# One stage for the input norm and the projections, one 264-column product for values and index weights, index scores between the projections

## The chip, the cores and the metric

The kernel runs on one core of one Trainium2 chip. The metric is the device time of one execution in microseconds (us), lower is better. TensorE is called PE in the profile, VectorE DVE, ScalarE ACT, GpSimd POOL, and SP is the engine that issues the loads.

## The reference, cut to what matters

One inference step of a two-layer encoder for 1024 new tokens of one stream and 32 tokens of a running one (1056 tokens, 1024 features, all float32). Layer 0 is attention in which an indexer picks 256 keys for each query; layer 1 is a gated linear recurrence. The change touches the beginning of layer 0 only:

```python
hn = rmsnorm(h, norm_w[0])
p = hn @ w_in                     # 1024 x 3720
q, k, v, z, qi, ki, wi = split_cols(p, [1024, 256, 256, 1024, 1024, 128, 8])
q, k, qi, ki = rope(q), rope(k), rope(qi), rope(ki)
idx_logits = einsum('bthd,bsd->bths', qi, ki)                    # 8 index heads
score = einsum('bth,bths->bts', wi * IDX_SCALE, relu(idx_logits))
_, sel = lax.top_k(score, n_sel)                                 # 256 (sample: 136) keys
```

After it come softmax attention over the selected keys, the output product, the recurrence and a final norm, which stay as they are. `v` is an output too.

## The kernel before

Tokens lie in nine tiles of 128 (the last has the 32 sample tokens). Products with weights are computed in split precision: each operand is a high part (a cast to fp32r) and a low part (the rest), and `product` (L181) adds three passes for each of the 8 slices of 1024 features, so one product is 24 matmuls.

**`input_norm` (L258)**, a block of its own. Per token tile: load x (three buffers; the load of tile t waits for tile t - 3 to be scaled), ACT squares and sums (L314), POOL turns the sum into a factor (`norm_stats_pool`, L239 and L242), DVE scales (L339), PE transposes eight 128x128 pieces (L365), and the transposed rows are multiplied by the norm weight and split into `hn_hi` and `hn_lo` (`split_normed` L173 and L176 on DVE, L305 on ACT). From t = 5 on ACT and POOL also split one of the first three weight tiles (`split_weights_hi` L208, `split_weights_lo` L215), POOL after the factor of the same t.

**`attention_project` (L370)**, the next block, goes through a list of units written out by hand. For the 30 weight tiles of 128 columns in the order KI, WI, QI0 to QI7, K0, K1, V0, V1, then Z and Q in turn, there are three units each (352 tokens a unit, weights stationary). The WI tile computes 128 columns for the eight index weights that it needs; they are transposed back by PE (L554) and copied by DVE (L748). V0 and V1 are done together in nine units, one for each token tile, tokens stationary and 256 columns moving. The index scores of all eight heads are one block of 96 units ahead of K1 (L560). A score unit is one float32 matmul of 272 to 512 columns, an ACT relu into one of two buffers (L607), and a DVE multiply-add into `score` (L758; L754 for head 0). PE may be four units ahead of their reader (four PSUM banks), ACT two units ahead of DVE:

```python
if i >= 4: pe.wait_ge(act_read, n_act[i - 3])
if s >= 2: act.wait_ge(scored, s - 1)
```

A rope unit has two ACT copies (L588, L589), a DVE product with cos (L739) and two POOL products and sums with sin (L641, L630). There are three slots for weights. SP loads tile c when PE is through with tile c - 3 (L464), and ACT and POOL split it after the unit that this line names:

```python
after.setdefault(min(last_of_tile[c - SLOTS] + 2, last_of_tile[c - 1]), []).append(c)
```

Once all scores are there, DVE searches each query's threshold bit by bit: `begin` and then 31 times propose, count over seven tiles (L714) and decide (L725, L726). It starts behind the first rope unit after the scores (K1's first), goes on between the last ropes and then by itself (L760 to L772). The attention block starts when all engines are done.

Of the kernel before, what the change touches and what calls it, by code (L numbers as in the profile page):

```python
# [16 lines left out]
ALU = mybir.AluOpType  # L17
# [8 lines left out]
P = 128  # L26
D = 1024
# [17 lines left out]
WI_TILE = WI0 + IH - P  # L45
W_SLOTS = 3

TILES = [KI0, WI_TILE] + [QI0 + P * i for i in range(IH)] + [K0 + P * i for i in range(2 * KVH)]
# [39 lines left out]
def build(nc, io):  # L88
    with ExitStack() as ctx:
# [37 lines left out]
        S["open"] = space("open_mask", [P, 3 * P])  # L127
        w_at = space.at
# [24 lines left out]
        input_norm(nc, S)  # L153
        attention_project(nc, S, space)
# [102 lines left out]

def input_norm(nc, S):  # L258

    io, sem, ps = S["io"], S["sem"], S["ps"]  # L260
    stats, half, ident, columns = S["stats"], S["half"], S["ident"], S["columns"]
    const_in, x_in = sem("const_in"), [sem(f"x_in{i}") for i in range(3)]
# [3 lines left out]
    act_hi_done = sem("hn_hi0_act")  # L266
# [6 lines left out]
    junk = space("junk", [P, D])  # L273
    with nc.Block() as block:  # L274
        @block.sync
        def _(sp):
            sp.dma_start(ident[:], io["ident"]).then_inc(const_in, 16)
            sp.dma_start(by_row[0:2 * KT], io["norm_w"].rearrange("l (k p) -> (l k) p", p=P)).then_inc(const_in, 16)
            sp.dma_start(by_row[2 * KT:3 * KT], io["rec_lb_logits"].rearrange("l (k p) -> (l k) p", p=P)).then_inc(const_in, 16)
            sp.dma_start(by_row[3 * KT:4 * KT], io["rec_gnorm_w"][0]).then_inc(const_in, 16)  # L280
            for t in range(NT):
                if t >= 3:
                    sp.wait_ge(xn_ready, t - 2)
                    sp.wait_ge(squares_ready, t - 2)
                sp.dma_start(xin[0:rows(t), t % 3, :], token_rows(io, t)).then_inc(x_in[t % 3], 16)

                c = t - FIRST_WEIGHT
                if 0 <= c < W_SLOTS:
                    sp.dma_start(S["w_raw"][:, c], w_in[:, :, TILES[c]:TILES[c] + P]).then_inc(S["raw_in"][c], 16)
            for name in ("cos", "sin", "limits"):  # L290
                sp.dma_start(S[name][:], io[name]).then_inc(S["tables_in"], 16)
            ck = cached_keys(S["score"])
            sp.dma_start(ck[:, :, 0:256], io["cache_k"][0, 0].rearrange("(b p) h d -> p b (h d)", p=P)).then_inc(S["cache_in"], 16)
            sp.dma_start(ck[:, :, 256:384], io["cache_kidx"][0, 0].rearrange("(b p) d -> p b d", p=P)).then_inc(S["cache_in"], 16)
            sp.dma_start(S["cv"][:], io["cache_v"][0, 0].rearrange("(b p) h d -> p b (h d)", p=P)).then_inc(S["cache_in"], 16)

        @block.scalar
        def _(act):
            def upper(t):

                act.wait_ge(columns_out, 1)
                act.wait_ge(tr_ready, 2 * t + 2)
                r = rows(t)
                for k in range(4):
                    last = act.activation(S["hn_hi"][:, 4 + k, span(t)], ps[2 * (t % 2) + 1][:, k * P:k * P + r],  # L305
                                          ACT.Copy, scale=columns[:, 0, 4 + k:5 + k])
                last.then_inc(act_hi_done, 1)

            for t in range(NT):
                r = rows(t)  # L310
                act.wait_ge(x_in[t % 3], 16 * (t // 3 + 1))
                if t:
                    act.wait_ge(squares_ready, t)
                act.activation(junk[0:r], xin[0:r, t % 3, :], ACT.Square,  # L314
                               accum_out=stats[0:r, 0, t:t + 1]).then_inc(squares_ready, 1)
                if t >= 2:
                    upper(t - 2)
# [1505 lines left out]
```

## Time and profile before

| | |
|---|---|
| median of three runs | 1551.94 us (1550.73 to 1554.93) |
| span of the profiled execution | 1547.9 us, 2.8 to 7.0 us under the three runs |
| busy in the span | PE 1402.9, DVE 965.9, ACT 560.5, POOL 508.8 us |
| input norm | 0 to 40 us |
| projections, scores, search | 40 to 492 us |
| everything after (not touched) | 492 to 1548 us |

The profiled execution has no time of its own beside its span; the runs' median lies 4.0 us above it. Times in the rows count from the start of the span.

### The profile page before, as it was taken

Reading aid. Unit: us, or ns where it says so; the run is one execution under the profiler, and the core shown is the slowest. Engines: PE = TensorE matmul, PEld = TensorE weight load, DVE = VectorE, ACT = ScalarE, POOL = GpSimd, SP = SyncE. Lnnn points to the kernel's source line nnn. Section 1 sums busy time; section 2 is a strip of 40 time slices with the busy share of each in tenths; the row PEclk is TensorE's granted clock in tenths of the full one; section 3 lists DMA queues with packets and bytes.
Section 4 is the critical chain, followed back from the end, with each engine's and each line's share of the span. In section 5 each row is a group of like instructions: output and inputs, shape, how many; then the busy total and the mean of one; then the engine's idle time right before and its main releaser. Section 6 shows DMA issues by size and latency. Waiting matters only on the chain. (4 is left out here: it accounts for less than half of the span.)

```text
span 1547.9 us, 21333 instructions
## 1 busy us (share of the span) xinstructions
PE 1402.9 (91%) x8109; PEld 1224.0 (79%) x8109; DVE 965.9 (62%) x1864; ACT 560.5 (36%) x1004; POOL 508.8 (33%) x404
## 2 busy tenths in 40 slices
PE   4999999999993899999979999999999999925898
PEld 3999647999992455548869999999999999914686
DVE  7011488999998989744550466475665566596332
ACT  6233463333322555541121444342525253340111
POOL 4276402355541001100020364544536163363000
PEclk9999999999996999999999999999999999957899
DMA  6121100232211410002231111010211110500221
GB/s 217 28 55 41 28 1 15 78 95 85 65 53 42 149 28 14 4 28 82 82 89 43 56 29 47 28 61 20 61 41 42 36 40 20 193 4 1 82 99 62
DMA packets 96180, 86.78 MB, mean 56 GB/s; under 512 B 4528, under 2 KB 84272, under 8 KB 96080
## 3 DMA queue, kind: packets, MB, share of 16 engines
q1 hardware_dynamic: 94448, 80.60, 16.9%
q0 software_dynamic: 1632, 4.82, 0.9%
q8 instruction: 66, 1.08, 0.3%
q14 instruction: 34, 0.28, 0.1%
HBM read 65.43 MB, written 19.97 MB: 55 GB/s over the span
## 5 line engine op out<-in xcount | busy, mean ns | idle before, releaser
L186 PE MATMUL bank<-hn_hi,rw_hi 128*128 128x352 f32 x768 | 250.3, 326 | 2.9 <-PEq L1009 2.9
L186 PE MATMUL bank<-hn_hi,rw_lo 128*128 128x352 f32 x768 | 247.2, 322 | 0.0
L186 PE MATMUL bank<-hn_lo,rw_hi 128*128 128x352 f32 x768 | 246.9, 322 | 0.0
L186 PE MATMUL bank<-hn_hi,w_hi 128*128 128x352 f32 x672 | 218.9, 326 | 3.6 <-PEq L274 3.6
L186 PE MATMUL bank<-hn_lo,w_hi 128*128 128x352 f32 x672 | 216.5, 322 | 0.0
L186 PE MATMUL bank<-hn_hi,w_lo 128*128 128x352 f32 x672 | 216.4, 322 | 0.0
L714 DVE TENSOR_SCALAR_CACHE_REDUCE marks<-score,bits 128x384 bf16<-128x384 f32 (+6 forms) x217 | 185.1, 917 | 3.7
L186 PEld LDWEIGHTS bank<-hn_hi,rw_hi 128*128 128x128 f32 x768 | 144.6, 188 | 4.6 <-POOL rw_lo L1145 3.1
L186 PEld LDWEIGHTS bank<-hn_lo,rw_hi 128*128 128x128 f32 x768 | 145.0, 189 | 0.0
L186 PEld LDWEIGHTS bank<-hn_hi,rw_lo 128*128 128x128 f32 x768 | 144.6, 188 | 0.0
L186 PEld LDWEIGHTS bank<-hn_hi,w_hi 128*128 128x128 f32 x672 | 127.0, 189 | 4.3 <-issue 3.7
L186 PEld LDWEIGHTS bank<-hn_lo,w_hi 128*128 128x128 f32 x672 | 127.2, 189 | 0.0
L186 PEld LDWEIGHTS bank<-hn_hi,w_lo 128*128 128x128 f32 x672 | 126.8, 189 | 0.0
L641 POOL TENSOR_TENSOR swapped<-swapped,sin 128x352 f32<-128x352 f32 x57 | 54.0, 947 | 187.8 <-ACT swapped L589 122.1
L1573 DVE TENSOR_TENSOR levels<-levels,q_rec 128x528 f32<-128x528 f32 (+1 forms) x48 | 101.4, 2177 | 1.9 <-ACT levels L1409 1.9
L843 PE MATMUL wide<-kT,q_tile 128*128 128x512 f32 (+3 forms) x192 | 75.4, 506 | 27.1 <-DMA q_tile<-q_rotated 26.9
L239 POOL TENSOR_SCALAR stats<-stats 128x1 f32<-128x1 f32 (+1 forms) x27 | 7.4, 273 | 279.4 <-ACT junk L1116 162.6
L1328 PE MATMUL wide<-levels 128*128 128x128 f32 (+1 forms) x832 | 98.2, 274 | 0.6
L1328 PEld LDWEIGHTS wide<-levels 128*128 128x128 f32 (+1 forms) x832 | 92.7, 185 | 6.0 <-issue 0.9
L1145 POOL TENSOR_TENSOR rw_lo<-rw_raw,rw_hi 128x1024 fp32r<-128x1024 f32 x32 | 76.0, 2386 | 59.6 <-ACT rw_hi L1138 59.5
L215 POOL TENSOR_TENSOR w_lo<-w_raw,w_hi 128x1024 fp32r<-128x1024 f32 x30 | 71.7, 2390 | 50.4 <-ACT w_hi L208 50.3
L843 PEld LDWEIGHTS wide<-kT,q_tile 128*128 128x128 f32 x192 | 36.6, 202 | 65.1 <-issue 34.2
(221 smaller groups left out, 2823.2 us busy)
## 6 DMA issues: line engine op xcount, KB each, us to landing
rw_raw<-in_rec_w_in SPq DMA_DIRECT2D x32, 512.0 KB, 4.1
w_raw<-in_att_w_in SPq DMA_DIRECT2D x30, 512.0 KB, 3.9
q_rotated<-relu SPq DMA_DIRECT2D x24, 176.0 KB, 1.9
xin<-in_x_prompt SPq DMA_DIRECT2D x8, 512.0 KB, 4.2
q_tile<-q_rotated SPq DMA_DIRECT2D x8, 512.0 KB, 3.7
wo_raw<-in_att_w_out SPq DMA_DIRECT2D x4, 1024.0 KB, 9.1
x_again<-in_x_prompt SPq DMA_DIRECT2D x8, 512.0 KB, 4.0
residual<-h_rows SPq DMA_DIRECT2D x8, 512.0 KB, 2.9
```

Source lines behind the costliest of these rows:

```text
L186: last = pe.matmul(out, l, r, start=n == 0, stop=n == len(passes) - 1)
L215: pool.tensor_tensor(S["w_lo"][:, slot], S["w_raw"][:, slot], S["w_hi"][:, slot].bitcast(F32), ALU.subtract).then_inc(S["w_lo_done"], 1)
L239: pool.tensor_scalar(stats[0:r, 1, t:t + 1], stats[0:r, 0, t:t + 1], 1.0 / D, EPS, ALU.mult, ALU.add).then_inc(pool_order, 1)
L641: pool.tensor_tensor(swapped[:, r % 3, :], swapped[:, r % 3, :], sin[:, part * CW:(part + 1) * CW], ALU.mult).then_inc(sin_done, 1)
L714: step(dve.tensor_scalar(marks[0:r, i % 2, 0:keys(t)], tile(i, t), bound, 0.0, op, ALU.add, accum_out=counts[0:r, first + i:first + i + 1]))
L843: last = pe.matmul(logits[0:rows(t), i % 2, a:e], q[:, t % 2, h, 0:rows(t)], src[:, h // GROUP, a:e], start=True, stop=True)
L1145: pool.tensor_tensor(S["rw_lo"][:, slot], S["rw_raw"][:, slot], S["rw_hi"][:, slot].bitcast(F32), ALU.subtract).then_inc(S["rec_lo_done"], 1)
L1328: last = pe.matmul(out[:, 0:r], left, right, start=True, stop=True)
L1573: dve.tensor_tensor(x, x, level_view(q[:, slot], m)[:, :, 1, :], ALU.mult).then_inc(q_scaled, 1)
```

## The change

The two blocks become one: each engine runs the instructions of the norm and goes on with the projections without a meeting of the engines. The norm weight is multiplied in on DVE together with the scale, from a copy that a load spreads over 128 partitions. Values and index weights are one product per token tile (tokens stationary, 264 columns moving), done in the norm's loop one tile behind the transposes. Their weights come in four loads ahead of x1, two of them with pieces of eight floats, and are split by ACT (after the first tile) and DVE. The WI tile, the V units and the transposes of the index weights are gone; 27 weight tiles stay. The index scores are no longer one block: the 12 units of head h stand ahead of weight tile QI(h+2), and those of heads 6 and 7 ahead of K0. The search starts behind K0's first unit, so K0 and K1 both lie behind the scores.

```diff
-TILES = [KI0, WI_TILE] + [QI0 + P * i for i in range(IH)] + [K0 + P * i for i in range(2 * KVH)]
+TILES = [KI0] + [QI0 + P * i for i in range(IH)] + [K0 + P * i for i in range(KVH)]
...
+    first, later = input_norm(nc, S), attention_project(nc, S)
+    with nc.Block() as block:
+        @block.sync
+        def _(sp):
+            first["sync"](sp)
+            later["sync"](sp)
...
+    def sync(sp):
+        sp.dma_start(ident[:], io["ident"]).then_inc(ident_in, 16)
+        for t in range(NT):
+            if t >= 3:
+                sp.wait_ge(xn_ready, t - 2)
+                sp.wait_ge(squares_ready, t - 2)
+            sp.dma_start(xin[0:rows(t), t % 3, :], token_rows(io, t)).then_inc(x_in[t % 3], 16)
+            if t == 0:
+                sp.dma_start(norm_w, io["norm_w"][0].partition_broadcast(P)).then_inc(norm_in, 16)
                 for g in range(2):
+                    ks = slice(4 * g, 4 * g + 4)
+                    sp.dma_start(wv_raw[:, ks, 0:KV], w_in[:, ks, V0:V0 + KV]).then_inc(wv_in[g], 16)
+                    sp.dma_start(wv_raw[:, ks, KV:VW], w_in[:, ks, WI0:WI0 + IH]).then_inc(wv_in[g], 16)
...
+    def scalar(act):
+        def upper(t):
+            for g in range(2):
+                act.wait_ge(tr_ready, 2 * t + g + 1)
+                act.copy(S["hn_hi"][:, 4 * g:4 * g + 4, span(t)], transposed(t, g)).then_inc(hi_done, 1)
+
+        def read_v(t):
+            act.wait_ge(v_ready, t + 1)
+            src = wide[token_block(t)[1], 2 + t % 2, :]
+            act.copy(S["v"][0:rows(t), t, :], src[:, 0:KV])
+            act.mul(S["wi"][0:rows(t), t, :], src[:, KV:VW], IDX_SCALE).then_inc(v_read, 1)
+
+        for t in range(NT):
+            r = rows(t)
+            act.wait_ge(x_in[t % 3], 16 * (t // 3 + 1))
...
+            act.activation(junk[0:r], xin[0:r, t % 3, :], ACT.Square,
+                           accum_out=stats[0:r, 0, t:t + 1]).then_inc(squares_ready, 1)
+            if t >= 1:
+                upper(t - 1)
+            if t == 1:
+                for g in range(2):
+                    ks = slice(4 * g, 4 * g + 4)
+                    act.wait_ge(wv_in[g], 32)
+                    act.copy(wv_hi[:, ks, :], wv_raw[:, ks, :]).then_inc(wv_hi_done, 1)
+            if t >= 3:
+                read_v(t - 3)
+            if 0 <= t - FIRST_WEIGHT - 2 < W_SLOTS:
+                split_weights_hi(act, S, t - FIRST_WEIGHT - 2)
...
+    def vector(dve):
+        def scale(t):
...
+            dve.scalar_tensor_tensor(xn[0:r, t % 2, :], xin[0:r, t % 3, :], stats[0:r, 2, t:t + 1],
+                                     norm_w[0:r], ALU.mult, ALU.mult).then_inc(xn_ready, 1)
+
+        dve.wait_ge(norm_in, 16)
+        scale(0)
+        for t in range(NT):
+            if t + 1 < NT:
+                scale(t + 1)
+            for g in range(2):
+                dve.wait_ge(hi_done, 2 * t + g + 1)
+                at = slice(4 * g, 4 * g + 4)
+                dve.tensor_tensor(S["hn_lo"][:, at, span(t)], transposed(t, g),
+                                  S["hn_hi"][:, at, span(t)].bitcast(F32), ALU.subtract).then_inc(lo_done, 1)
+            if t == 0:
+                for g in range(2):
+                    ks = slice(4 * g, 4 * g + 4)
+                    dve.wait_ge(wv_hi_done, g + 1)
+                    dve.tensor_tensor(wv_lo[:, ks, :], wv_raw[:, ks, :], wv_hi[:, ks, :].bitcast(F32),
+                                      ALU.subtract).then_inc(wv_lo_done, 1)
...
+            if t >= 1:
+                m = t - 1
+                pe.wait_ge(lo_done, 2 * m + 2)
+                if m == 0:
+                    pe.wait_ge(wv_lo_done, 2)
+                if m >= 2:
+                    pe.wait_ge(v_read, m - 1)
+                product(pe, wide[:, 2 + m % 2, 0:VW],
+                        [lambda k, x=x: x[:, k, token_block(m)[0]] for x in (S["hn_hi"], S["hn_lo"])],
+                        [lambda k, x=x: x[:, k, :] for x in (wv_hi, wv_lo)]).then_inc(v_ready, 1)
...
+    def head_scores(h):
+        return [("score", h, piece, t) for t in itiles for piece in range((keys(t) + 511) // 512)]
+
     units = []
     for c, col in enumerate(tiles):
-        if col == K0 + P:
-            for t in itiles:
-                for piece in range((keys(t) + 511) // 512):
-                    units += [("score", h, piece, t) for h in range(IH)]
...
+        if QI0 + 2 * P <= col < KI0:
+            units += head_scores((col - QI0) // P - 2)
+        if col == K0:
+            units += head_scores(IH - 2) + head_scores(IH - 1)
...
+                    if part == 0 and t == itiles[0]:
+                        pe.wait_ge(rope_done, 3 * (c + 2))
...
-                if kind != "score" and n_score[i] > 0:
+                if kind != "score" and n_score[i] == n_score[N]:
```

The `product`, `split_weights_hi`, `split_weights_lo` and `norm_stats_pool` that it calls are those of before.

## Rows read from the trace of the kernel before

**Rows 1.** The page, part 2: busy tenths in 40 slices of 38.7 us.

```profile
PE   4999999999993899999979999999999999925898
...
DVE  7011488999998989744550466475665566596332
...
PEclk9999999999996999999999999999999999957899
```

**Rows 2.** Windows by stage: start:end, length, busy us (instructions) by engine, clock, DMA share, GB/s.

```profile
40.00:170.00 130.00, 130.00 (x805) 129.76 (x805) 15.22 (x29) 39.28 (x74) 75.22 (x71) 1.00 0.15 41
...
174.00:244.00 70.00, 69.63 (x193) 31.23 (x193) 57.04 (x92) 46.46 (x94) 2.40 (x2) 0.98 0.00 1
...
250.00:470.00 220.00, 218.16 (x1431) 217.31 (x1430) 213.39 (x509) 67.24 (x133) 105.00 (x90) 1.00 0.24 69
470.00:492.00 22.00, 0.00 (x0) 0.00 (x0) 21.26 (x57) 1.16 (x3) 3.77 (x5) 0.55 0.07 25
```

**Rows 3.** Timeline, end of the search: start us, us, engine, line, operation, tiles.

```profile
485.05 0.17 DVE L725 TENSOR_TENSOR bits<-counts,select_state 128x7 uint32<-128x7 f32 x1
...
491.76 0.17 DVE L725 TENSOR_TENSOR bits<-counts,select_state 128x7 uint32<-128x7 f32 x1
```

**Rows 4.** Timeline, start of the search behind K1's first unit.

```profile
248.12 0.45 ACT L588 COPY swapped<-bank 64x352 f32<-64x352 f32 x1 [2.05 <-PE bank L186]
...
249.05 0.52 DVE L739 TENSOR_TENSOR kT<-bank,cos 128x352 f32<-128x352 f32 x1 [2.28 <-ACT swapped L589]
...
249.53 0.07 DVE L684 MEMSET counts<- 128x14 f32 x1
```

**Rows 5.** Timeline, input norm: squares of tiles 0 and 2; a split, the factor behind it.

```profile
5.71 1.06 ACT L314 ACTIVATE junk<-xin 128x1024 f32<-128x1024 f32 x1 [3.70 <-DMA xin<-in_x_prompt]
...
8.96 1.06 ACT L314 ACTIVATE junk<-xin 128x1024 f32<-128x1024 f32 x1 [0.84 <-DMA xin<-in_x_prompt]
...
25.30 2.36 POOL L215 TENSOR_TENSOR w_lo<-w_raw,w_hi 128x1024 fp32r<-128x1024 f32 x1
...
27.75 0.51 POOL L239 TENSOR_SCALAR stats<-stats 128x1 f32<-128x1 f32 x1
```

**Rows 6.** Timeline: twelve transposes at full clock; copies of two V units in a row.

```profile
53.92 1.39 PEld L512 LDWEIGHTS wide<-ident,score 128*128 128x128 f32 x12
...
258.59 0.37 ACT L601 COPY v<-bank 128x256 f32<-128x256 f32 x1 [1.94 <-PE bank L186]
...
261.45 0.37 ACT L601 COPY v<-bank 128x256 f32<-128x256 f32 x1 [2.48 <-PE bank L186]
```

**Rows 7.** Groups by line and shape, last stage: busy us, mean ns.

```profile
L1738 DVE SCALAR_TENSOR_TENSOR y<-h_again,stats,final_w 128x1024 f32<-128x1024 f32 x8 | 10.3, 1285 | 17.5 <-POOL stats L242 17.5
```

**Rows 8.** Windows of 5 us: cold start of the projections; one weight load of 512 KB.

```profile
40.00:45.00 5.00, 5.00 (x17) 5.00 (x18) 0.00 (x0) 0.00 (x0) 0.59 (x3) 1.00 0.02 3
...
255.00:260.00 5.00, 5.00 (x43) 5.00 (x42) 4.79 (x14) 1.27 (x3) 0.94 (x1) 1.00 0.40 108
```

**Rows 9.** The page, part 6: loads of weight tiles, KB each, us to landing.

```profile
w_raw<-in_att_w_in SPq DMA_DIRECT2D x30, 512.0 KB, 3.9
```

**Rows 10.** Timeline, first score units: a weight split meets a score.

```profile
176.57 1.04 ACT L208 CAST w_hi<-w_raw 128x1024 fp32r<-128x1024 f32 x1
...
177.69 2.35 POOL L215 TENSOR_TENSOR w_lo<-w_raw,w_hi 128x1024 fp32r<-128x1024 f32 x1 [3.63 <-ACT w_hi L208]
...
178.03 2.42 DVE L758 SCALAR_TENSOR_TENSOR score<-relu,wi,score 128x384 f32<-128x384 f32 x1 [0.70 <-ACT relu L607]
```

**Rows 11.** Timeline: runs of seven scores on DVE, 512 and 272 columns.

```profile
184.78 5.89 DVE L758 SCALAR_TENSOR_TENSOR score<-relu,wi,score 128x512 f32<-128x512 f32 x7 [0.24 <-ACT relu L607]
...
237.82 4.05 DVE L758 SCALAR_TENSOR_TENSOR score<-relu,wi,score 32x272 f32<-32x272 f32 x7 [0.25 <-ACT relu L607]
```

**Rows 12.** Timeline: weight loads of two float32 records of 512 columns, full clock.

```profile
560.74 0.19 PEld L843 LDWEIGHTS wide<-kT,q_tile 128*128 128x128 f32 x1 [0.24 <-issue]
...
561.17 0.19 PEld L843 LDWEIGHTS wide<-kT,q_tile 128*128 128x128 f32 x1 [0.24 <-issue]
```

More of the change, by code:

```diff
@@ L127, in build @@
         S["open"] = space("open_mask", [P, 3 * P])
+        v_at = space.at - (3 * P + sum(keys(t) for t in range(2, NT)) - PAST // P * 384) * 4
+        S["wv_raw"] = Space(nc, v_at)("wv_raw", [P, KT, VW])
+        S["wv_lo"] = Space(nc, v_at)("wv_lo", [P, KT, VW], F32R)
         w_at = space.at
@@ new lines, in transposed @@
+    def transposed(t, g):
+        return ps[2 * (t % 2) + g][:].rearrange("p (k q) -> p k q", k=4)[:, :, 0:rows(t)]
+    def scalar(act):
[11 more added lines that the diff above has]
+            act.wait_ge(x_in[t % 3], 16 * (t // 3 + 1))
+            if t:
+                act.wait_ge(squares_ready, t)
+            act.activation(junk[0:r], xin[0:r, t % 3, :], ACT.Square,
[11 more added lines that the diff above has]
+                split_weights_hi(act, S, t - FIRST_WEIGHT - 2)
+        upper(NT - 1)
+        for t in range(NT - 3, NT):
+            read_v(t)
@@ L358, in _, with tensor @@
+    def tensor(pe):
+        pe.wait_ge(ident_in, 16)
+        for t in range(NT + 1):
+            if t < NT:
                 r = rows(t)
@@ L414, in attention_project @@
     n_score = [sum(u[0] == "score" for u in units[:i]) for i in range(N + 1)]
-    last_wi = max(i for i, u in enumerate(units) if u[0] == "wi")
     first_score = next(i for i, u in enumerate(units) if u[0] == "score")
     last_of_tile = {u[1]: i for i, u in enumerate(units) if u[0] != "score"}
-    second_v = tiles.index(V0) + 1
-    last_of_tile[second_v] = last_of_tile[second_v - 1]
-    assert (second_v - 1) % SLOTS + 1 == second_v % SLOTS
     after = {}
@@ L425, in attention_project @@
         after.setdefault(min(last_of_tile[c - SLOTS] + 2, last_of_tile[c - 1]), []).append(c)
-    v_last = max(i for i, u in enumerate(units) if u[0] == "v")
-    rows_before = {v_last + 4 + 3 * t: t for t in range(NT)}
+    first_gate = min(i for i, u in enumerate(units) if u[0] == "gate")
+    rows_before = {first_gate + 3 + 3 * t: t for t in range(NT)}
     def rotated(i):
@@ L457, in attention_project, with sync @@
     ck = cached_keys(score)
-    wiT = score[0:DEC, 2048:2048 + T]
-    with nc.Block() as block:
-        @block.sync
-        def _(sp):
+    if True:
+        def sync(sp):
             def load(c):
@@ L655, in _, with vector @@
             add_sine()
-        @block.vector
-        def _(dve):
+        def vector(dve):
             n_order = 0
```

206 lines of the change are left out of this document (81 added, 125 removed).

## The prediction, made before the changed kernel was run

> **What bounds the kernel now.** I read the slices first [rows 1]: PE is busy nearly everywhere except at the start and in the thirteenth slice, where it idles, the clock column dips and DVE is full. So the end of the projection block belongs to DVE. The windows say it exactly [rows 2]: from 470 to 492 PE does nothing while DVE works 21.3 of 22 us. The timeline shows what it does there: whole bits of the search, 6.71 us from decision to decision, the last at 491.8 [rows 3], and the next block starts behind it. Going back, DVE is 213 of 220 us busy from 250 to 470 [rows 2]: the search is one unbroken run from 249.5 [rows 4], and nothing that PE does beside it counts. So the figure to forecast is not PE's total work. It is **the time at which the search begins**, and that is the time at which K1's first unit comes through: PE began it one unit (3.8 us) before ACT's copy at 248.1, at 244.2, and the search starts 5.3 us after that [rows 4].
>
> What lies ahead of it: 40 us of norm; 33 units from 40 to 170; four us for the index weights and a wait; the score block, 70 us for 96 units [rows 2]. 805 records less 12 cache transposes and one beyond the end are 792 matmuls, 33 units of 24; without 1.4 us of transposes [rows 6] and 2.3 us of cold start (17 matmuls in the first 5 us, where 0.159 us each would give 31 [rows 8]) a unit is 126.3 / 33 = 3.82 us. In the score block DVE sets the pace: seven scores of 512 columns take 5.89 us, seven of 272 take 4.05 [rows 11], which is 0.84 and 0.58 each, 1.08 ns for each further column. A head has 12 pieces and 4768 columns: 12 x 0.58 + 1504 x 0.00108 = 8.6 us, with the gaps 70 / 8 = 8.8. PE needs less: two records for each score, a record of 512 columns 0.43 us [rows 12], so 1.68 ns a column and 8.0 us a head.
>
> **The change part by part.**
>
> *Removed ahead of the search:* the WI tile and K0's move behind the scores, 6 units x 3.82 = 22.9 us; the 4 us from 170 to 174; the norm's 40 us and the 2.3 us of cold start, which come back below in another form. The V units and K1 were behind the start of the search, under DVE's cover: V's 9 x 2.86 us [rows 6] leave PE there, but PE already had 22 us of idle time at the end [rows 2], so that removal is worth nothing. Now the same work stands ahead of the search. This is the main thing against the change.
>
> *The first stage.* The x loads landed at 5.7 (tile 0) and 9.0 (tile 2) [rows 5], 1.6 us for each 512 KB. Three small loads go from the front, so I put x0 at 4.5. Ahead of x1 now stand the spread norm weight (512 KB, 1.6 us) and the weights of V (1.06 MB, 3.3 us) with 1024 pieces of 32 bytes. For those pieces I have no row. Below they cost nothing beyond their bytes; a weight load is 1024 pieces of 512 bytes and keeps the 16 engines 0.40 x 5 = 2.0 us busy [rows 8]. I take 2.0, being nearest in count, and 4.0 as the upper end. x1 lands at 4.5 + 1.6 + 3.3 + 2.0 + 1.6 = 13.0. Behind it hang, on ACT: squares (1.15 with the read of the sum), the two copies of tile 0 (1.15, an estimate from the 0.37 us for 256 columns [rows 6]), two casts of V's weights (2.1, from 1.04 for 1024 columns [rows 10]), to 17.4. On DVE: the scale of tile 1 with two SBUF inputs, which takes 1.285 us in the last stage [rows 7]; two low parts (1.4); two low parts of V's weights (2.5, in the size of the same row). The first product can start at about 20.3. It runs cold: 17 matmuls of 352 columns in 5 us [rows 8] are 0.22 us for 264 columns, 5.3 us in all, to 25.6. That repays the cold start saved at 40.
>
> After that PE has, per tile, eight transposes (8 x 1.39 / 12 = 0.93) and a product of 24 (2.86 x 264 / 256 = 2.95) [rows 6], 3.9 us, and less transposing for the last: 25.6 + 8 x 3.9 - 0.7 = 56.1. In the tiles where weights are split, POOL's factor waits for the 2.36 us split ahead of it [rows 5], then come the 1.3 us scale and 1.4 us of low parts on DVE. Laid out in time, three tiles take about 4.5 us in place of 3.9: projections start at **57.5**, range 55 to 62. Against 42.3 (40 and the cold start) that is 15.2 us later.
>
> *The scores between projections.* Here the intended gain is PE's 8.0 in place of DVE's 8.8 us a head, since DVE's lag is made up under the next rope units. But the rule for splits ("two units after the tile that frees the slot") was harmless with units of 3.8 us, and now the two units are scores. Take X as the end of the last rope unit. The slot becomes free at X and its load lands 3.9 us later [rows 9]. ACT does two relus (to 2.3), then stands before the cast until X + 4.05, and ends it at 5.15 (the cast takes 1.04 [rows 10]). PE has its four banks of lead, used up at 3.85. Relus go on at 5.65, but POOL's split runs from 5.25 to 7.6, and the third score wants to start on DVE at 5.65. What happens then stands in the trace: a score that arrived 0.34 us behind the start of such a split took 2.42 us in place of 0.7, and ended 0.4 us behind POOL's end [rows 10]. So the third score ends at 7.95; ACT may be only two ahead, so PE's seventh and eighth score pass, but the ninth waits until 8.6; from there all go at DVE's pace. PE may start the next rope unit when the ninth is read: with scores ending at 8.6, 9.3, 10.05 and 10.85, at **11.6 us**, not 8.0. DVE ends at 14.5, ahead of the next rope at 15.4, so nothing is carried over. Head 0 has a cheaper first operation: 11.1. Heads 6 and 7 stand together and share a split: 11.6 + 8.8 = 20.4. The sum is 11.1 + 5 x 11.6 + 20.4 = 89.5 us, against 70 before: 19.5 us more.
>
> The Trainium skill ("SBUF — State Buffer", section "Who interferes with whom") says that a DVE instruction with two SBUF inputs and a GpSimd instruction that reads SBUF exclude each other for the whole instruction; the 2.42 us agree. By it the new scale with two inputs can be held up by a split in the same way. Its page "DMA: Bandwidth & Descriptors" (Specifications) puts the smallest transfer at line rate at 512 bytes, which speaks for a price of the 32-byte pieces; no row here shows one.
>
> *Sum.* K0's first unit starts at 57.5 + 27 x 3.82 (103.1) + 1.4 + 89.5 = 251.5, against 244.2: **+7.3 us**. The search starts 5.3 us later as before. K0's three ropes are now inside DVE's run, 3 x 0.52 [rows 4] = +1.6. DVE has no gap in K0 and K1 since `begin` alone (12 us from 249.5) leaves it behind. POOL has about as much to do beside the search as before (five more rope units, three splits fewer), so I change nothing for collisions; the range covers 2 us of it. All after the search is unchanged. Together +8.9 us on a span of 1547.9: 1556.8, and with the 4.0 us that the median lies above the span, **1560.8 us**, 0.6% slower. About 0.3%, 4.7 us, is what a measurement of this kernel can tell from no change.
>
> **The rivals.**
>
> *Faster: the waits in the bursts are absorbed.* If transfer and split fall where PE's four banks cover them, a burst costs PE's 8.0: 64 in place of 89.5, 1535. For it speaks that nothing in PE's own work is more than that, against it the 3.9 us and the 2.42 us row. It decides at the length of a burst: at 10.3 us each (seven bursts, 1.27 us less in each) the change is even, below 9.7 it is faster beyond 0.3%. Time between 1535 and 1547; chance 0.20.
>
> *No difference: only the transfer is waited for.* If the split misses the scores (the score gets in ahead of POOL), a burst is 8.0 + 1.9 = 9.9, seven bursts save 12 us: 1549. With only some bursts hit, up to 1556. Chance 0.20.
>
> *Slower, by the first stage.* The 32-byte pieces take 4 us or more and the splits chain through POOL: projections start at 62, 1565. Chance 0.08.
>
> *Slower still, by the clock.* PE stands twice in each burst, 1.9 and 1.35 us. The clock column fell to 0.55 in 22 us of idle time [rows 2], and the cold rate is about half. If it falls in bursts, each is up to 1.7 us longer: 1572. Chance 0.07.
>
> **How the numbers follow.** My forecast holds 0.45, for itself 1557 to 1565. Slower is 0.45 + 0.08 + 0.07 = 0.60, same 0.20, faster 0.20. The low end, 1541, leaves out the better part of the absorbed case (0.08), the high end, 1570, the clock case and a tail of the first stage (0.10).
>
> **What would show it.** Projections start at 55 to 62 and not near 45. In each burst ACT stands before its cast behind a transfer, and one score takes 2 us or more behind a split. PE has two gaps in each, a burst is 11 to 12 us, the double one 20 to 21. The search begins near 257 and ends near 500, PE's idle time ahead of the attention block is 30 to 40 us in place of 22. The prediction is wrong if bursts are 8 to 9 us long, if the first product starts near 14, or if the search itself gets shorter or longer by more than 3 us.

## The result, and the profile after

The changed kernel takes **1554.65 us** (median of 15 runs, 1554.05 to 1556.6), the kernel before 1551.24 us in the same comparison (15 runs, 1549.74 to 1554.93). The ratio is 1.0021, 95% interval 1.0014 to 1.0029: 3.4 us slower, where 8.9 us (0.6%) were forecast. The time lies inside the range, 6 us below the forecast. The change is below the 4.7 us that the prediction called distinguishable, but the whole interval lies above 1. The span of the profiled execution is 1552.8 us, 4.9 over before.

The 4.0 us from span to median that the prediction carried over were of two kinds. In every recorded run of the kernel before that lists its span, the time is 1.8 to 2.1 us above it. So the execution of 1547.9 us was one of about 1549.9, 1.3 us under the median of the fifteen runs and 2.0 under that of the three. In the runs of the changed kernel the distance is 1.8 to 1.9 us.

The page's slices, against [rows 1]: PE has its idle slice at the same place, and DVE is no longer idle at the start.

```profile
PE   6998899999981899999979999999999999925898
DVE  4235548999998998744550466574665566596332
PEclk9999999999995999999999999999999999957899
```

The windows by stage, columns as in [rows 2]: the scattered scores (105 to 235), the double burst, the search, and the end of the search.

```profile
105.00:235.00 130.00, 115.45 (x551) 88.29 (x550) 62.74 (x81) 53.12 (x106) 50.05 (x42) 1.00 0.09 25
235.00:251.00 16.00, 14.49 (x45) 6.64 (x44) 13.91 (x20) 9.57 (x19) 1.56 (x1) 1.00 0.00 1
255.00:490.00 235.00, 204.37 (x1291) 203.56 (x1289) 227.58 (x558) 67.05 (x131) 112.41 (x99) 0.94 0.21 60
490.00:500.40 10.40, 0.00 (x0) 0.00 (x0) 6.21 (x16) 1.28 (x1) 0.24 (x1) 0.50 0.24 67
```

In 130 us PE is idle for 14.6. The clock column says 1.00 there, and behind the burst shown below the matmuls of 352 columns start every 0.16 us again from their second on: the waits in the bursts cost no clock. Behind 490 PE waits for DVE, as before: the search still sets the end, and its start is still what counts.

The first stage, timeline of both kinds of work, against [rows 5]:

```profile
11.81 1.06 ACT L364 ACTIVATE relu<-xin 128x1024 f32<-128x1024 f32 x1 [5.97 <-DMA xin<-in_x_prompt]
...
13.91 1.28 DVE L395 SCALAR_TENSOR_TENSOR xn<-xin,stats,swapped 128x1024 f32<-128x1024 f32 x1 [5.65 <-POOL stats L244]
13.94 2.06 ACT L372 CAST wv_hi<-wv_raw 128x1056 fp32r<-128x1056 f32 x2
...
16.31 2.42 DVE L412 TENSOR_TENSOR wv_lo<-wv_raw,wv_hi 128x1056 fp32r<-128x1056 f32 x2
...
18.87 0.56 PE L188 MATMUL wide<-wv_hi,hn_hi 128*128 128x264 f32 x1 [1.66 <-DVE wv_lo L412]
```

Squares of tile 1 begin when x1 has landed, at 11.81 (forecast 13.0). The first product starts 1.4 us before its forecast of 20.3, and the last before the projections ends at 55.24 (forecast 57.5).

One burst, from the end of the rope unit at 114.01 to the next at 125.39; the timeline of PE, ACT, DVE and POOL, against [rows 10]:

```profile
114.01 4.03 PE L620 MATMUL bank<-kiT,qiT_zT_gT 128*128 128x384 f32 x12
114.21 0.37 SPq L532 DMA_DIRECT2D w_raw<-in_att_w_in  x1
...
115.14 1.17 ACT L662 ACTIVATE relu<-bank 128x384 f32<-128x384 f32 x2
...
117.94 1.04 ACT L210 CAST w_hi<-w_raw 128x1024 fp32r<-128x1024 f32 x1 [1.62 <-DMA w_raw<-in_att_w_in]
118.89 0.76 ACT L662 ACTIVATE relu<-bank 128x320 f32<-128x320 f32 x2
119.06 2.35 POOL L217 TENSOR_TENSOR w_lo<-w_raw,w_hi 128x1024 fp32r<-128x1024 f32 x1 [0.39 <-ACT w_hi L210]
119.35 7.79 DVE L807 SCALAR_TENSOR_TENSOR score<-relu,wi,score 128x320 f32<-128x320 f32 x8 [1.47 <-ACT relu L662]
119.37 1.77 PE L620 MATMUL bank<-kiT,qiT_zT_gT 128*128 128x448 f32 x4 [1.32 <-ACT relu L662]
121.84 0.49 ACT L662 ACTIVATE relu<-bank 128x384 f32<-128x384 f32 x1 [2.20 <-DVE score L807]
122.39 1.98 PE L620 MATMUL bank<-kiT,qiT_zT_gT 128*128 128x512 f32 x4 [1.25 <-ACT relu L662]
...
125.39 0.43 PE L188 MATMUL bank<-hn_hi,w_hi 128*128 128x352 f32 x1
```

This is the forecast burst line by line: two relus, ACT in front of its cast for the transfer (1.62 us), POOL's split from 119.06, the third score meeting it (ACT stands 2.20 us for its buffer), and two PE gaps of 1.3 us (the first was forecast at 1.9). It lasts 11.4 us, forecast 11.6.

The start and the end of the search, timeline, against [rows 4] and [rows 3]; K0's first unit and the last decision:

```profile
249.46 0.43 PE L188 MATMUL bank<-hn_hi,w_hi 128*128 128x352 f32 x1
...
495.91 0.17 DVE L778 TENSOR_TENSOR bits<-counts,select_state 128x7 uint32<-128x7 f32 x1
...
500.47 0.79 PE L894 MATMUL wide<-kT,q_tile 128*128 128x128 f32 x2 [39.97 <-DMA q_tile<-q_rotated]
```

The search begins at 255.05 (memset at L737) and decides last at 495.91, 240.9 us later; before it was 242.2 us [rows 3, 4]. PE stands for 40 us ahead of the first matmul of the attention block (last row), the last 4.6 of them behind the search; 30 to 40 were forecast.

### The profile page after: what moved, and what is told of

It is laid out like the page before. It is cut to its first block and busy times, and to the rows that moved or that the text cites. A ratio compares the mean times of both kernels' runs of the same rounds, so it can differ in the third digit from the quotient of the medians.

```text
span 1552.8 us, 21064 instructions
## 1 busy us (share of the span) xinstructions
PE 1387.3 (89%) x8028; PEld 1208.6 (78%) x8028; DVE 973.3 (63%) x1801; ACT 557.2 (36%) x991; POOL 507.1 (33%) x401
## 5 line engine op out<-in xcount | busy, mean ns | idle before, releaser
L188 PE MATMUL bank<-hn_hi,w_hi 128*128 128x352 f32 x648 | 210.6, 325 | 0.0
L188 PE MATMUL bank<-hn_hi,w_lo 128*128 128x352 f32 x648 | 208.0, 321 | 0.0
L188 PE MATMUL bank<-hn_lo,w_hi 128*128 128x352 f32 x648 | 207.9, 321 | 0.0
L188 PEld LDWEIGHTS bank<-hn_hi,w_hi 128*128 128x128 f32 x648 | 121.6, 188 | 3.3 <-ACT relu L662 3.3
L188 PEld LDWEIGHTS bank<-hn_lo,w_hi 128*128 128x128 f32 x648 | 121.9, 188 | 0.0
L188 PEld LDWEIGHTS bank<-hn_hi,w_lo 128*128 128x128 f32 x648 | 121.5, 188 | 0.0
L894 PE MATMUL wide<-kT,q_tile 128*128 128x512 f32 (+3 forms) x192 | 74.7, 502 | 40.2 <-DMA q_tile<-q_rotated 40.0
L1020 ACT ACTIVATE probs<-probs,low 128x128 f32<-128x128 f32 (+8 forms) x72 | 55.6, 772 | 87.2 <-DVE low L980 86.9
```

What stands on the lines that cost most here:

```text
L188: last = pe.matmul(out, l, r, start=n == 0, stop=n == len(passes) - 1)
L894: last = pe.matmul(logits[0:rows(t), i % 2, a:e], q[:, t % 2, h, 0:rows(t)], src[:, h // GROUP, a:e], start=True, stop=True)
L1020: act.activation(probs[0:r, i % RING, 0:n], probs[0:r, i % RING, 0:n], ACT.Exp, scale=-1.0, bias=low[0:r, 0, i:i + 1], accum_out=low[0:r, ...
```

## The experiments

Below, "start" is the start of the projections, "begin" the first memset of the search, and "scores" what the score units add ahead of the search: begin - 5.3 - start - 104.5 (27 units, 103.1, and the cache's transposes, 1.4). By it the changed kernel's scores cost 90.0. Each ratio is against runs of the kernel before on the same chip. The times are medians of runs; start, begin, scores and search come from the one profiled execution of each kernel.

| kernel | us | ratio to before | start | begin | scores | search |
|---|---|---|---|---|---|---|
| before | 1551.24 | 1 | 40.0 | 249.5 | 70 | 242.2 |
| changed | 1554.65 | 1.0021 [1.0014, 1.0029] | 55.2 | 255.0 | 90.0 | 240.9 |
| e1 both splits behind the scores | 1538.14 | 0.9917 [0.9902, 0.9932] | 54.7 | 236.0 | 71.5 | 242.0 |
| e2 POOL's split alone behind | 1545.79 | 0.9964 [0.9951, 0.9977] | 54.8 | 243.6 | 79.0 | 242.0 |
| e3 both six scores later | 1540.60 | 0.9931 [0.9916, 0.9946] | 54.9 | 239.8 | 75.1 | 240.9 |
| e4 scores as one block | 1535.61 | 0.9903 [0.9887, 0.9920] | 55.5 | 236.9 | 71.6 | 240.8 |
| e5 no 32-byte pieces | 1554.85 (one run) | - | 55.0 | 254.7 | 89.9 | 241.0 |
| e6 e1 with x1 first | 1534.63 | 0.9888 [0.9873, 0.9903] | 52.3 | 233.8 | 71.7 | 241.7 |
| e8 before, K0 behind the scores | 1546.00 | 0.9957 [0.9942, 0.9972] | 40.2 | 239.7 | - | 247.4 |
| e9 e1 with scores in groups of four | 1537.46 | 0.9905 [0.9888, 0.9921] | 54.9 | 237.2 | 72.5 | 241.8 |
| e10 eight columns moving | 1577.05 (one run) | - | 76.4 | 277.5 | 91.3 | 240.9 |
| e11 e6, groups one unit later | 1530.42 | 0.9864 [0.9848, 0.9881] | 51.4 | 229.7 | 68.5 | 242.0 |
| e12 136 columns moving | 1567.15 | 1.0097 [1.0064, 1.0130] | 64.9 | 266.0 | 91.3 | 240.8 |
| e13 e11, PE busy ahead | 1529.97 | 0.9858 [0.9841, 0.9874] | 49.9 | 228.2 | 68.5 | 241.7 |

**Are the waits behind the splits the cost of the scores?** e1 puts ACT's cast and POOL's split after the second rope unit that follows:

```diff
-        after.setdefault(min(last_of_tile[c - SLOTS] + 2, last_of_tile[c - 1]), []).append(c)
+        later = [i for i, u in enumerate(units) if u[0] != "score" and i > last_of_tile[c - SLOTS]]
+        after.setdefault(min(later[1], last_of_tile[c - 1]), []).append(c)
```

> Only the place of the weight splits moves: a split that fell on the second score of a burst now stands behind the second rope unit after the burst, for ACT and POOL alike. Theory (a burst is stretched by the wait for the transfer and by the DVE score that meets POOL's split): a burst falls from about 11.6 us to PE's own 8.0 to 8.3, eight heads from 90 to 64-67, the search begins at 229 to 232 us of the span in place of 255, and the kernel takes 1528 to 1533 us. Rival (bursts are long because short runs of scores refill four banks and two relu buffers each time, and DVE's own 8.8 us a head sets the pace): little changes, a burst stays at 10 us or more and the time at 1545 us or above.

e2 uses the new rule for POOL's split alone, ACT's cast stays two units behind:

```diff
+        after_lo.setdefault(min(later[1], last_of_tile[c - 1]), []).append(c)
...
-                for c in after.get(i, []):
+                for c in after_lo.get(i, []):
```

> ACT's cast stays on the second score of a burst, and so does its wait for the transfer; only POOL's subtraction (2.4 us) moves behind the second rope unit after the burst. Theory: the transfer wait alone leaves one gap of 1.9 us, a burst is 9.9 us in place of 11.6, seven of them save 12 us: 1541 to 1545 us. If the collision with POOL counted for nothing: 1554 to 1555. If it were everything: 1530.

e3 puts both behind the eighth score instead of the second, where the load has long landed but the split still meets scores:

```diff
+        free = last_of_tile[c - SLOTS]
+        after.setdefault(free + 8 if units[free + 1][0] == "score" else min(free + 2, last_of_tile[c - 1]), []).append(c)
```

> Cast and subtraction stay inside the burst but six scores later, when the transfer has landed. The transfer wait is gone, the collision of POOL's subtraction with DVE's scores stays. Theory: a burst is 9.5 to 10 us, since DVE still loses about 1.7 us to a blocked score and then goes on at its own pace; 1540 to 1545 us, and one score in each burst of 2 us or more. If only the transfer wait counted: 1530.

The search begins 19.1 us earlier in e1 and the time falls by 16.5: the waits were there, and they were 18.5 of the 90 us. The three kernels share them out. Changed to e2, 11.0 us: POOL's split off the scores. In e2 ACT still waits 12.0 us in 7 times for transfers. From e2 to e1, 7.5 us: that wait. e3 has no such wait left. In each of its bursts the split meets one of the last scores (2.48 us in the burst from 110), most of that falls under the next rope unit, and a burst takes 9.2 us against e1's 8.95. Only the double burst, where more scores follow, pays for it: 19.6 us against 17.8, with a relu that waits 2.1 us. The shares hold for this order of taking the waits away; no run takes away the transfer's alone and leaves the split on the third score. e3 came out in its range, e2 0.8 us above it.

e1 missed its 1528 to 1533, because a burst does not fall to PE's 8.0 us. Timeline of e1's burst, which runs from 110.19 to 119.14:

```profile
110.52 5.46 PE L621 MATMUL bank<-kiT,qiT_zT_gT 128*128 128x384 f32 x15
...
111.69 0.93 POOL L696 TENSOR_TENSOR swapped<-swapped,sin 128x352 f32<-128x352 f32 x1
111.84 10.24 DVE L808 SCALAR_TENSOR_TENSOR score<-relu,wi,score 128x384 f32<-128x384 f32 x12
112.58 2.57 POOL L685 TENSOR_TENSOR qiT_zT_gT<-qiT_zT_gT,swapped 128x352 f32<-128x352 f32 x2
113.13 0.44 ACT L663 ACTIVATE relu<-bank 128x320 f32<-128x320 f32 x1 [0.64 <-DVE score L808]
114.46 0.44 ACT L663 ACTIVATE relu<-bank 128x320 f32<-128x320 f32 x1 [0.90 <-DVE score L808]
115.59 0.49 ACT L663 ACTIVATE relu<-bank 128x384 f32<-128x384 f32 x1 [0.70 <-DVE score L808]
```

The twelve scores take 10.24 us, not 8.6: the first three or four meet the products and sums with sin that POOL still owes the rope unit before. They hold relus up by 0.6 to 0.9 us, and a head costs 71.5 / 8 = 8.9 us where 8.0 was expected. That these collisions are the 0.9 us is argued from the rows; no run moves POOL's rope work away.

**Is the interleaving worth anything then?** e4 leaves the stage as changed and gathers the scores in the block of before:

```diff
+            for t in itiles:
+                for piece in range((keys(t) + 511) // 512):
+                    units += [("score", h, piece, t) for h in range(IH)]
```

> The interleaving alone is undone: all 96 scores in one block ahead of K0, in the order of the kernel before (tile, piece, then head); the norm stage and the 264-column product stay. Theory: the block costs DVE's 70 us and about 2 for one split in it, against 90 for the interleaved scores, so the search begins at 236 to 238 us and the kernel takes 1534 to 1538 us: the interleaving as it was written costs 18 us where it was to bring 5. Rival (interleaving helps, and the time was lost in the first stage and by the values ahead of the search): 1557 us or more.

It came out as expected. Its scores cost 71.6 us, as in e1 (71.5), and as before (70): twelve in a row between projections, even without their waits, gain nothing over one block. So the rest of the change was worth 1% by itself (K0's move alone, e8 below, 0.4%), and the interleaving as it was placed cost 19.0 us (1554.65 less 1535.61), that 1% and 0.2% more.

e9 places four scores of head h behind each rope unit of the weight tile that follows its own, with e1's rule:

```diff
+                if QI0 + P <= col < KI0:
+                    units += head_scores((col - QI0) // P - 1)[4 * part:4 * part + 4]
```

> On top of the splits behind the bursts: the 12 units of head h stand in three groups of four, one behind each rope unit of QI(h+1); only head 7 stands by itself ahead of K0. Theory (a burst of 12 is longer than PE's 8.0 because DVE, at 8.8 us and more beside POOL's rope work, uses up the four banks): groups of four fit in the banks, PE goes at its own 8.0 us a head, 66 us for all in place of 71.5, and the search begins 4 to 6 us earlier than with bursts, at 230 to 232; 1532 to 1534 us. Rival (every score meets POOL's rope work now, and DVE is blocked more often): 1538 us or more.

The middle heads cost 8.3 us: PE spends 7.8 on the scores of a head, and each of the three returns to 352 columns adds 0.15 to 0.2. But the whole missed its 1532 to 1534 us and shows no difference from e1: the first score of head 0 waited 3.0 us for POOL to finish that head's queries, and head 7 stood alone. e11 starts one unit later, places all scores from one list and has x1 first (e6):

```diff
+    waiting = [u for h in range(IH) for u in head_scores(h)]
...
+            for part in range(3):
+                units.append(("rope", c, part, target))
+                if QI0 + P <= col < KI0 and (col, part) != (QI0 + P, 0):
+                    units += waiting[:4]
+                    del waiting[:4]
```

> Splits behind the scores, x1 loaded ahead of V's weights, and scores in groups of four behind each rope unit from QI1's second to QI7's last; the last 16 units stand ahead of K0. Head 0 then no longer waits 3 us for POOL's sum, with PE's half rate behind it. 80 units at PE's pace of 8.3 us a head take 55 us and 16 at DVE's 11.7, 67 in all: the search begins at 229 to 230 us in place of 233.8, and the time is 1530 to 1532, the fastest of the study. If the collisions with POOL's rope work cost as much as they save, it is that of the version with bursts and x1 first, 1534.6 or more.

The windows of e11 ahead of the search: PE has no idle time left.

```profile
52.00:225.00 173.00, 173.00 (x855) 136.02 (x854) 96.15 (x120) 79.17 (x160) 73.65 (x63) 1.00 0.12 34
```

The busy column alone does not tell e11 from e1, whose PE is busy 177.0 of the 178 us from 57 to 235, though its scores cost 3 us more. The distance from one weight tile's scores to the next tells them apart: 20.0 us in e11, 20.5 in e1, for the same three rope units and twelve scores.

The scores cost 68.5 us against e6's 71.7, and the kernel takes 1.36% less than before, as expected. The intended gain is there in the trace; in the runs the intervals of e11 and e6 overlap. That a group of four fits PE's lead of four banks is the reason argued for it, and other sizes were not tried.

**The first stage.** e5 loads the 264 columns behind V in one load per half, without the pieces of eight floats; it leaves out the index weights of the reference (these eight columns come from elsewhere). e6 is e1 with the loads of V's weights behind that of x1 (`if t == 1:`).

> The changed kernel with the loads of 32-byte pieces left out: each half of V's weights comes in one load of 264 neighbouring columns, so the index weights are computed from the wrong columns. If the 1024 small pieces cost what I took (2.0 us), x1 lands at 9.8 in place of 11.8 us and the projections start 2 us earlier, near 53. If they cost nothing beyond their bytes, x1 lands within 0.3 us of 11.8.

> On top of the splits behind the bursts: the load of x1 goes ahead of V's weights. x1 lands about 3.5 us earlier, at 8 to 8.5 us, and the norm of tile 1 with it, but the first product waits for the weights' split, whose loads land 1.6 us later. If the first product (18.8 us) hangs on the chain behind x1, it starts at about 17 and all follows 1 to 2 us earlier: 1536 to 1537. If it hangs on the weights: no difference, 1538.

In e5 the squares of tile 1 begin at 11.30 in place of 11.81, the first product at 18.36 in place of 18.87, and the one run says no difference. In the eight kernels with the pieces and this order of loads the squares begin at 11.72 to 12.00, so the step is clear of their scatter: 1024 pieces of 32 bytes cost about 0.5 us, not 2.0. In e6 squares of tile 1 begin at 8.26 and the first product at 15.32 (expected near 17); the search begins 2.2 us earlier than in e1, and the time fell by 0.29% of before.

e10 and e12 were to price the values ahead of the search. In e10 only the eight index-weight columns move (no values are computed, copies of the index weights are stored in their place); in e12 the second 128 value columns move too (the first 128 are left out). All loads and splits stay.

```diff
-                product(pe, wide[:, 2 + m % 2, 0:VW],
+                product(pe, wide[:, 2 + m % 2, KV:VW],
```

> The changed kernel with the 256 value columns left out of the product per token tile: 8 columns move in place of 264, and v gets copies of the index weights, so v and what attention makes of it are not the reference's. The loads and the split of V's weights stay. It prices the values that now stand ahead of the search. Theory (PE sets the pace of the stage once the first product starts, 3.9 us a tile): the first product still starts at 18.8 us, then the norm's own chain of about 3 to 3.4 us a tile sets the pace, and the projections start at 45 to 47 in place of 55, the time falls 8 to 10 us, to 1545 to 1547. Rival (the stage is bound by its loads and the norm's chain anyway, and the values are free there): projections at 53 or later, 1553 or more.

> The changed kernel with 136 columns moving in each token tile's product, the second half of the value columns and the index weights; the first 128 value columns are not computed (the second half is stored in their place). All loads, casts and low parts stay. It prices value columns while TensorE is kept busy. Theory (columns set the pace): 24 products every 0.121 us with 264 columns become 24 at about 0.065 us with 136, 1.3 us less in each of eight tiles, 10 us less ahead of the projections: they start near 45, the search near 245, time 1544 to 1546. Rival 1 (weight loads set the pace): 8 columns were one every 0.213 us at the low clock, so half of that, 0.107 us, at the high clock: 0.3 us less in a tile, projections at 52 to 53, time 1552. Rival 2 (few columns keep the clock low, as with 8 columns): 24 every 0.213 us until the 352-column units begin, projections at 70 or later, time 1570 or more.

Less work, and 22 us slower (one run): both theories fell in e10. Timeline of PE in e10 at its last such products and the first projections:

```profile
75.72 0.35 PE L188 MATMUL wide<-wv_hi,hn_hi 128*128 128x8 f32 x1
75.93 0.35 PE L188 MATMUL wide<-wv_lo,hn_hi 128*128 128x8 f32 x1
76.15 0.35 PE L188 MATMUL wide<-wv_hi,hn_lo 128*128 128x8 f32 x1
76.36 0.64 PE L188 MATMUL bank<-hn_hi,w_hi 128*128 128x352 f32 x1
76.80 0.49 PE L188 MATMUL bank<-hn_lo,w_hi 128*128 128x352 f32 x1
...
79.44 0.42 PE L188 MATMUL bank<-hn_lo,w_hi 128*128 128x352 f32 x1
79.69 0.33 PE L188 MATMUL bank<-hn_hi,w_lo 128*128 128x352 f32 x1
79.86 0.32 PE L188 MATMUL bank<-hn_hi,w_hi 128*128 128x352 f32 x1
```

Matmuls of 8 columns start every 0.213 us although nothing holds them up, and those of 352 first every 0.29, then every 0.16 from 79.7: PE was at the lower of its two levels (1.2 GHz) through all its value products and the first 3 us of 352-column ones. A tile of transposes and 8-column products takes 6.7 us at this level. The changed kernel went up at 23.2, in its first tile's product (one matmul every 0.22 us before, every 0.12 behind).

e12 shows both levels. Timeline of PE at 28 us, and the windows from 40 on:

```profile
28.07 0.27 PE L188 MATMUL wide<-wv_hi,hn_lo 128*128 128x136 f32 x1
28.18 0.28 PE L188 MATMUL wide<-wv_hi,hn_hi 128*128 128x136 f32 x1
28.29 0.27 PE L188 MATMUL wide<-wv_lo,hn_hi 128*128 128x136 f32 x1
```

```profile
40.00:45.00 5.00, 4.30 (x35) 3.78 (x34) 3.02 (x4) 4.06 (x9) 4.78 (x4) 1.00 0.74 236
45.00:50.00 5.00, 2.91 (x16) 2.57 (x17) 5.00 (x6) 1.48 (x4) 3.12 (x6) 0.79 0.00 0
50.00:55.00 5.00, 5.00 (x28) 4.81 (x28) 0.91 (x4) 0.57 (x3) 0.00 (x0) 0.50 0.02 3
...
60.00:65.00 5.00, 5.00 (x25) 5.00 (x25) 0.00 (x0) 0.45 (x2) 0.00 (x0) 0.50 0.00 0
65.00:70.00 5.00, 5.00 (x23) 5.00 (x23) 0.00 (x0) 0.44 (x2) 0.00 (x0) 0.66 0.00 0
70.00:75.00 5.00, 5.00 (x34) 5.00 (x32) 0.53 (x1) 1.49 (x4) 0.94 (x1) 1.00 0.01 3
```

At the full level (2.4 GHz) a matmul of 136 columns starts every 0.111 us, one of 264 every 0.121. The Trainium skill ("TensorE: Matmul & The Clock Gate", section "LDWEIGHTS (loading the stationary operand)") gives the time of a weight load in ns as its columns divided by 1.2, which makes 107 ns of 128 columns, an estimate. At the full level 0.111 us for a load and a matmul of 136 columns agrees with it, and so does the nearly flat price; at the lower level the same pair took 0.213 us. In e12's trace 128 value columns cost 0.010 us in each of 216 matmuls, 2.2 us in all: the first rival was right about the pace. The level had risen at 27.3, 8.5 us into the value products. Then PE stood 2.5 us for a scale on DVE (after 44.3), the clock fell to 0.50 and stayed there through 16 us of busy 136-column products, up to the 352-column ones. The start of 64.9 lies between the two rivals, 53 and 70, since a part of the stage ran at each level. Its ten runs lie between 1557.2 and 1579.8 us, so this time is no price of columns at all. e12 has one trace, which does not say where the other nine runs rose or fell.

e13 turns it round: e11 with seven products of the identity by itself, 256 columns wide and read by nobody, in PE's idle time ahead of the first value product.

```diff
+                pe.matmul(wide[:, 3, 0:2 * P], ident[:], ident[:].unsqueeze(1).to_broadcast([P, 2, P]),
+                          start=True, stop=True)
```

> The fastest version (groups of four scores one unit later, x1 first) with seven float32 products of the identity by itself, 256 columns wide, whose output nobody reads: four before the first transposes, one between those of tiles 0 and 1, two behind them, in TensorE's idle time. Theory (the low clock at the first value product comes from what TensorE did before it): the level is high at the first product, its 24 matmuls take 2.9 us in place of 4.5, the search begins near 228 in place of 229.7, time 1528 to 1529. Rival (the level rises only behind the first stretch without a gap, which still starts at the first product): no difference, 1530.4, or up to 1 us more if the added products are still running when the operands are ready.

Timeline of PE in e13 before and in the first value product:

```profile
13.43 1.91 PE L422 MATMUL wide<-ident 128*128 128x256 f32 x4
15.20 0.59 PE L188 MATMUL wide<-wv_hi,hn_hi 128*128 128x264 f32 x1
15.59 0.35 PE L188 MATMUL wide<-wv_lo,hn_hi 128*128 128x264 f32 x1
15.77 0.28 PE L188 MATMUL wide<-wv_hi,hn_lo 128*128 128x264 f32 x1
15.89 0.28 PE L188 MATMUL wide<-wv_hi,hn_hi 128*128 128x264 f32 x1
```

The first product now runs every 0.12 us from its third matmul on; in e11 it ran every 0.22 for its first fifteen. Projections and search begin 1.6 and 1.5 us earlier. The intervals of e11 and e13 overlap, so the runs do not show the 0.5 us between their medians, and 1528 to 1529 was missed; the trace shows the step. It bears the theory out, that the level at the first product comes from what PE did before it.

**Does an earlier search stay as short?** e8 is the kernel before with one edit, so that K0 follows the scores:

```diff
-        if col == K0 + P:
+        if col == K0:
```

> The kernel before with one edit: the block of scores stands ahead of K0 in place of K1. Theory (only the start of the search counts, and three more rope products on DVE cost 1.6 us in it): the search begins 11.5 us earlier, near 238, and the kernel takes 9 to 11 us less, 1541 to 1543. Rival (PE's work or the projections' end counts): no difference.

The search begins 9.8 us earlier but lasts 247.4 us, 5.2 longer, and only 6.6 us arrive in the time, where 9 to 11 were expected. The groups by line show where: three more ropes on DVE (1.6 us) and the small instructions of the search. First e8, then the changed kernel (busy us, mean ns):

```profile
L725 DVE TENSOR_TENSOR bits<-counts,select_state 128x7 uint32<-128x7 f32 x31 | 21.5, 695 | 1.1
L726 DVE COPY_PREDICATED bits<-bits 128x7 uint32<-128x7 uint32 x31 | 9.6, 311 | 1.1
```

```profile
L778 DVE TENSOR_TENSOR bits<-counts,select_state 128x7 uint32<-128x7 f32 x31 | 16.4, 531 | 1.1
L779 DVE COPY_PREDICATED bits<-bits 128x7 uint32<-128x7 uint32 x31 | 7.4, 239 | 1.1
```

Undisturbed such an instruction takes 0.17 us [rows 3]. With the one that proposes a bit (10.3, 11.0 us) their sums are 41.4 us in e8, 34.8 in the changed kernel, 37.6 before. With the timelines of DVE and POOL laid side by side, nearly every one of these 93 small instructions that takes longer than 0.25 us runs beside a POOL instruction. The kernels differ in those that meet a weight split: 14 in e8 (14.9 us beyond the 0.17 each), 12 before (10.2), 9 in the changed kernel (7.8), 9 in e1 (8.6). POOL has 17, 16, 15 and 16 splits there, so the number of splits alone does not order them; the phase between the two engines is what is left, and no run tests it by itself.

The length of the search is steady for one placement of the splits. It is 240.8 to 241.0 us in the six kernels with the new first stage that split by the rule of before or by e3's, and 241.7 to 242.0 in the six whose POOL splits by e1's, with one split more beside the search.

## Why the prediction was wrong in size

**What bounds the kernel: right.** The last decision of the search sets what follows. In e1 the search begins 19.05 us earlier and lasts 1.1 longer, and the span falls by 18.0. The medians are less exact, 16.5 us (e2: 11.5 us earlier, 8.9 faster), since they and the trace are of different executions. Behind the last decision no kernel is changed, and yet this part takes from 1055.6 (e4) to 1059.4 us (e11) in the traces. So an account from traces holds for the part up to the last decision, and differences of up to 4 us behind it can be scatter.

**The first stage, +15.2 us: measured +12.9, the term was 2.3 too large.** 1.4 us is the first product's start, mostly the 2.0 us for the 32-byte pieces, "nearest in count" to a weight load's 1024 pieces, which e5 puts at 0.5. Another 0.3 is the colder product (5.0, not 5.3), and 0.5 the rest of the stage (31.4, not 31.9), where PE waited 0.5 us for the chain of splits in place of 1.4. A tile took 3.8 us at best (forecast 3.9): the product 3.0 (2.95), its eight transposes 0.8 (0.93). But 3.0 us is not the price of the values: with eight columns 24 matmuls took 5.1 us at the lower level, so half of that, 2.6, is an estimate for the full one. By it the values moved ahead of the search cost about 3 us at the full level (216 matmuls, 0.121 less 0.107 each), and PE reached that level at 23 us, during them; in e10, which leaves them out, it did at 79. The prediction counted the slow start, and had no term for how long it lasts.

**The scores, 89.5 us: measured 89.7** (K0's first unit at 249.46 less the start 55.24 and 104.5), nearly each step of the burst as written, and e1 to e3 show its two waits to be the cause. PE's matmuls give the bursts as 11.4 us for head 0 (forecast 11.1), 11.4 to 11.6 for the next five (11.6) and 20.4 for the double one (20.4); that the sum is met to 0.2 is in part luck. The Trainium skill ("SBUF — State Buffer", "Who interferes with whom") says of a DVE instruction with two SBUF inputs and a GpSimd one that reads SBUF that they exclude each other for the whole instruction; the 2.20 us for which ACT waited behind POOL's 2.35, and the 10.24 us of e1, agree.

**Search begins +7.3: measured +5.5** (249.53 to 255.05). The 5.3 us from K0's unit to the search were 5.6. They were 5.5 before too: K1's first unit began at 243.99, where the prediction took 244.2 from ACT's copy.

**The search, +1.6: measured -1.4. This is the step that failed most, 3.0 us.** "I change nothing for collisions": the three small instructions cost 2.8 us less than before, against 1.5 us for the ropes. The same sum is 3.8 us above before in e8, so a shift of some microseconds either way was in it, and the 2 us that the range allowed were too few. Its count of POOL's work beside the search, "five more rope units, three splits fewer", was off as well: the traces have three more and one fewer (15 for 16). The collisions with splits fell from 12 to 9; that this comes from the phase against POOL's work is argued from where the time lies, and was not tested by itself.

**The sum.** The last decision came 4.15 us later, forecast 8.9: 2.3 from the first stage, 3.0 from the search, less 0.5 in the steps between. Behind it the span gained 0.75 more, which is within the scatter there. The medians differ by 1.5 us less than the spans, mostly because the profiled execution of before was about 1.3 us faster than its median and that of the changed kernel only 0.1.

**The rivals.** "The waits are absorbed" did not happen, and its 64 us for the scores was out of reach for bursts of twelve: free of both waits they cost 71.5. "Only the transfer is waited for" gave 1549, and the kernel that does just that, e2, took 1545.79; its single bursts last 9.8 to 10.0 us, the rival's 9.9. The clock did not fall in the bursts (1.00 from 105 to 251, and one matmul every 0.16 us behind the burst at 114).

## What to carry to other kernels

Work placed between units of a known length inherits every rule that counts in units: "two units later" was 7.6 us and became 1.3, and the cast and the split landed on a transfer and on the other engine's two-input instructions. Interleave in groups that the buffers' lead can take (four scores for four banks here; other sizes were not tried), and measure the mixture against one block. When a stage is priced by its columns, ask first at which clock level it runs and what paces it: here 128 columns cost 0.010 us a matmul, and the kernel without them took 12.5 us longer (e12, a median of runs that scatter by 22 us), the one without all 256 value columns 22 us longer (e10, one run).

## What had not been expected of the hardware

- PE stayed at its lower level in e10 from 20 to 76 us, busy all the time with transposes and 8-column products (0.213 us each), and rose 3.1 us after its first 352-column product. In the changed kernel it rose 4.3 us after the first 264-column product, in e12 8.5 us after the first 136-column one. At the full level a stop of 2.5 us in e12 was followed by the fall, and it stayed low through the next 16 us of 136-column products. The page's clock column showed 1.00 in e10 all the while; the spacing of the matmuls told the level.
- 1024 pieces of 32 bytes, loaded beside 1 MB of large ones, cost 0.5 us (e5).
- The deciding DVE instruction on 7 elements, 0.17 us alone, averaged 0.53 to 0.70 us over 31 rounds beside POOL.
- The part behind the search, the same in every kernel, took between 1055.6 and 1059.4 us.
